# Two value products side by side, and two differential scores side by side, in the attention of a two-layer hybrid trunk

## The reference

```python
h = x @ w_in
q_lat, ckv, krope, g_mla, dq, dk, dv, g_diff = _split_cols(h, EVEN_SECTIONS)

# latent attention: one softmax map a head, values from the compressed latent
s = einsum('bqhc,bkc->bhqk', q_abs, ckv) + einsum('bqhr,bkr->bhqk', q_rope, krope)
p = softmax(where(_chunk_mask(qpos, kpos), s * MLA_QK_DIM ** -0.5, NEG_INF))
o_lat = einsum('bhqk,bkc->bqhc', p, ckv)        # then times w_uv, head by head

# differential attention: two maps a head, the second subtracted
s = einsum('bqhid,bkhid->bhiqk', dq, dk) * DIFF_HD ** -0.5      # DIFF_HD = 64
p = softmax(where(_chunk_mask(qpos, kpos), s, NEG_INF))
a = p[:, :, 0] - lam * p[:, :, 1]
o_diff = einsum('bhqk,bkhe->bqhe', a, v)

o = concatenate([o_mla * silu(g_mla), rmsnorm(o_diff) * silu(g_diff)]) @ w_out
y = layernorm(ALPHA * x + o)
```

## Time and profile before

| | us |
|---|---|
| median of 3 runs | 844.55 (844.47 to 845.53) |
| the profiled execution, its own time | 844.67 |
| its span, first to last instruction | 842.9 |
| TensorE busy | 813.1 (96%) |
| VectorE busy | 524.9 (62%) |
| ScalarE busy | 412.1 (49%) |

### The profile page before, as it was taken

The page is one execution under the profiler, slowest core; times in us unless marked ns, Lnnn a source line. Parts: engine busy times, 40 slices in busy tenths (PEclk is TensorE's granted clock), DMA queues, the critical chain, the costliest instruction groups (busy, mean ns, idle before and its releaser), DMA issues.

```text
span 842.9 us, 17104 instructions
## 1 busy us (share of the span) xinstructions
PE 813.1 (96%) x6676; PEld 707.9 (84%) x6676; DVE 524.9 (62%) x1045; ACT 412.1 (49%) x945; POOL 74.8 (9%) x102
## 2 busy tenths in 40 slices
PE   6999999999999999999999999999999999999995
PEld 6996688888888899778899998888988888887674
DVE  4265355665665657766942565666577676778877
ACT  4233533334444456532324555675566665687710
POOL 2120000100000000000310010001100110121002
PEclk9999999999999999999999999999999999999998
DMA  7631211211323334514133334333332333334103
GB/s 234 153 97 50 75 44 52 64 49 42 121 77 105 112 97 134 158 61 137 57 124 109 114 101 140 92 106 110 128 101 91 127 126 115 117 125 132 60 30 125
DMA packets 67533, 86.25 MB, mean 102 GB/s; under 512 B 6016, under 2 KB 53920, under 8 KB 67456
## 3 DMA queue, kind: packets, MB, share of 16 engines
q1 hardware_dynamic: 63712, 74.47, 28.7%
q0 software_dynamic: 3744, 10.70, 4.0%
HBM read 74.25 MB, written 10.90 MB: 101 GB/s over the span
## 4 chain that ended last, share of the span: by engine, by line
PE 80%; issue 9%; DVE 5%; ACT 4%; POOL 2%; DMA 1%; SPq 0%; DVEq 0%; POOLq 0%; ACTq 0%
PE turn L955 24%; PE pair L955 17%; PE value L955 16%; PE proj L955 15%; PE turn L995 3%; PE turn L1171 2%; POOL rstd L928 1%; PE value L995 1%; PE proj L995 1%; PE proj L1171 1%; DVE w_lo L1604 1%; ACT w_hi L1371 1%; DMA x_sb<-in_x_prompt_dram 1%; PE pair L995 1%; DVE probs L1719 0%
## 5 line engine op out<-in xcount | busy, mean ns | idle before, releaser
L1604 DVE TENSOR_TENSOR w_lo<-stage,w_hi 128x512 fp32r<-128x512 f32 (+1 forms) x136 | 91.9, 682 | 114.4 <-ACT w_hi L1371 114.0
L955 PE MATMUL turn<-w_hi,xT_hi 128*128 128x256 f32 (+2 forms) x340 | 106.0, 312 | 1.0 <-DVE xT_lo L1609 0.7
L955 PE MATMUL turn<-w_hi,xT_lo 128*128 128x256 f32 (+2 forms) x340 | 102.5, 301 | 0.0
L955 PE MATMUL turn<-w_lo,xT_hi 128*128 128x256 f32 (+2 forms) x340 | 102.4, 301 | 0.0
L1371 ACT CAST w_hi<-stage 128x512 fp32r<-128x512 f32 (+1 forms) x144 | 87.4, 616 | 19.2 <-PE value L955 6.5
L955 PEld LDWEIGHTS turn<-w_hi,xT_hi 128*128 128x128 f32 x340 | 64.8, 191 | 3.7 <-DVE x_sb L1851 1.5
L955 PEld LDWEIGHTS turn<-w_hi,xT_lo 128*128 128x128 f32 x340 | 64.8, 191 | 2.5
L955 PEld LDWEIGHTS turn<-w_lo,xT_hi 128*128 128x128 f32 x340 | 64.9, 191 | 2.1
L1451 ACT ACTIVATE work<-pair,peak 128x512 f32<-128x512 f32 (+4 forms) x80 | 40.9, 516 | 46.2 <-DVE peak L1708 46.1
L1719 DVE TENSOR_TENSOR_SCAN probs<-probs 128x512 f32<-128x512 f32 (+4 forms) x80 | 61.4, 801 | 1.6
L955 PE MATMUL value<-w_hi,xT_hi 128*128 128x256 f32 (+2 forms) x194 | 60.1, 310 | 0.7 <-DVE w_lo L1604 0.7
(11 more groups left out here) (535 smaller groups left out, 2079.6 us busy)
## 6 DMA issues: line engine op xcount, KB each, us to landing
stage<-in_w_in_odd_dram SPq DMA_DIRECT2D x64, 256.0 KB, 2.7
stage<-in_w_in_even_dram SPq DMA_DIRECT2D x44, 256.0 KB, 2.8
k_c<-in_cache_sb_k_dram SPq DMA_DIRECT2D x32, 256.0 KB, 3.5
v_c<-in_cache_sb_v_dram SPq DMA_DIRECT2D x32, 256.0 KB, 2.9
mlaK<-in_cache_diff_k_dram SPq DMA_DIRECT2D x8, 512.0 KB, 4.1
mlaK<-in_cache_diff_v_dram SPq DMA_DIRECT2D x8, 512.0 KB, 4.5
stage<-in_w_out_even_dram SPq DMA_DIRECT2D x16, 256.0 KB, 2.6
stage<-in_w_out_odd_dram SPq DMA_DIRECT2D x16, 256.0 KB, 2.6
```

The lines of the kernel that those rows point to most:

```text
L955: return nc.tensor.matmul(o, l, r, start=first, stop=last)
L1604: v.tensor_tensor(piece(w_lo[:, sec % 2, words]), piece(stage[:, n % STAGES, :]), piece(w_hi[:, sec % 2, words].bitcast(F32)), ALU.subtrac ...
```

## The change

Two edits of the list, and one helper in TensorE's code.

- "value" of the first latent prompt step of a two (M 3 or M 2) is put off by one turn. It then stands directly ahead of the "value" of its neighbour (M 0 or M 1). There are eight such twos.
- Where two differential prompt steps stand next to each other (`firsts`: D (3, 0), (3, 3), (2, 1), (2, 3), (1, 1) and (0, 2)), the 64-row products of both come first (two jobs "rows"), then the masks of both, all at the first step's turn. The second step's score is thus a turn earlier. The code of the products is moved into `diff_scores`; the number of products does not change. The order on VectorE, ScalarE and SyncE follows the list.

```diff
--- before.py
+++ after.py
@@ -72,13 +72,24 @@
     def weighted(s):
         return [("turn", s)] + ([("turn2", s)] if s[0] == "M" else [])
 
+    heads = [i for i, s in enumerate(steps) if s[0] == "D"]
+    firsts = [i for i in heads if i + 1 in heads and (heads.index(i) == 0 or i - 1 not in heads)]
+
+    def values(i):
+
+        kinds = steps[i][0] + steps[i + 1][0] if i + 1 < len(steps) else ""
+        return [] if kinds == "MM" else [i - 1, i] if i and steps[i - 1][0] + steps[i][0] == "MM" else [i]
+
     for i, now in enumerate(steps):
-        jobs.append(("score", now))
+        if i in firsts:
+            jobs += [("rows", now), ("rows", steps[i + 1]), ("score", now), ("score", steps[i + 1])]
+        elif i - 1 not in firsts:
+            jobs.append(("score", now))
         between = fills.get(i, [])
         if now[0] == "MS":
             jobs += flat_jobs(between)
-        if i >= 3:
-            s = steps[i - 3]
+        for n in values(i - 3) if i >= 3 else []:
+            s = steps[n]
             jobs.append(("value", s))
             for turns_on, job in after(s):
                 later.setdefault(i + turns_on, []).append(job)
@@ -995,6 +1006,16 @@
                     i = nc.tensor.transpose(ps(job)[0:c, c0:c0 + r], src, ident[0:r, 0:r])
                 i.then_inc(filled[where[job][0]], 1)
 
+            def diff_scores(s):
+
+                _, t, h = s
+                for j in range(t + 1):
+                    wait_drained(pe, ("dkT", j, h // 2))
+                wait_drained(pe, ("dqT", t, h // 2))
+                for i in range(2):
+                    r = slice(HD * i, HD * i + HD)
+                    mm(ps(("score", s))[:, i, 0:width(s)], dqT[t][r, h, :], dkT[r, h, 0:width(s)], True, False)
+
             pe.wait_ge(consts_in, 16)
             for job in schedule:
                 kind = job[0]
@@ -1073,11 +1094,15 @@
                     pe.wait_ge(kc_in[b % 2], 16 * (4 * g + b // 2 + 1))
                     transposes(job, [((2 * i + half) * P, k_c[:, b % 2, half, i * P:(i + 1) * P])
                                      for i in range(2) for half in range(2)])
+                elif kind == "rows":
+                    wait_bank(pe, ("score", job[1]))
+                    diff_scores(job[1])
                 elif kind == "score":
                     s = job[1]
                     n = width(s)
-                    wait_bank(pe, job)
                     o = ps(job)
+                    if ("rows", s) not in schedule:
+                        wait_bank(pe, job)
                     if s[0] == "M":
                         _, t, pair = s
                         pe.wait_ge(kr_done, PT_TILES)
@@ -1104,13 +1129,8 @@
                         mm(o[:, 0:PAST], qrb, kr_cT[0:QK, b % 2, :], False, False)
                         mm(o[:, PAST:n], qrb, krTs[0:QK, b * NEW:(b + 1) * NEW], False, True).then_inc(done, 1)
                     elif s[0] == "D":
-                        _, t, h = s
-                        for j in range(t + 1):
-                            wait_drained(pe, ("dkT", j, h // 2))
-                        wait_drained(pe, ("dqT", t, h // 2))
-                        for i in range(2):
-                            r = slice(HD * i, HD * i + HD)
-                            mm(o[:, i, 0:n], dqT[t][r, h, :], dkT[r, h, 0:n], True, False)
+                        if ("rows", s) not in schedule:
+                            diff_scores(s)
                         for i in range(2):
                             m = mm(o[:, i, n - P:n], identb[:, :], mask_chunk[:, :], False, True)
                         m.then_inc(done, 1)
```

## The result

The changed kernel takes 838.82 us (four runs, 837.91 to 839.20) against 844.51 before (844.47 to 845.53): ratio 0.9928, 95% interval 0.9911 to 0.9945. Run again beside the experiments it took 838.05 against 844.54, ratio 0.9925 (0.9913 to 0.9938). It is faster, by 5.7 and by 6.5 us. Forecast were 840.0 and a gain of 4.6.

The account below looks back on a forecast made before the run. TensorE, busy for 96% of the span, was taken to bound the kernel. Terms of 1.84, 0.43, 1.56 and 0.73 sum to 4.56 us off the median 844.55, forecasting 840.0 us, range 838.6 to 842.3.

Parts of the forecast that it names:

- borders of eight value visits: Latent value products: eight twos each save one entry to and exit from 64-column weights, 0.23 us each, 1.84 us.
- wait at the first visit: First round, value of M (3, 0): its wait for VectorE's copy of its transposed weights goes, 0.43 us.
- waits of four light steps: Ends of M (0, 1), M (0, 2), M (1, 2), M (1, 3): put-off values fill TensorE's idle time before sample scores, 1.56 us.
- scores of six twos: Differential scores: paired steps save way in and slow product behind masks, 0.15 us in each of four twos; 0.73 us in all.
- so this stays: Transposes behind a value visit: the first one's 0.16 us instead of 0.11 was taken to remain, as behind masks.
- hangs on a chain: Light step M (0, 1): VectorE's last cache copy was said to follow the last projection through ScalarE's copy, rotation and weights' conversion.
- There I find nothing that becomes late: Full steps: a projection of 2.9 us stands before every such need, so no time change was counted.
- The 0.85 stays: Score (2, 0), 384 columns: its four 64-row products were to take 0.85 us in the new place too.
- it is paid inside the mode as well: Differential 64-row products: some 0.1 us of uncovered weight load in each pass was to remain without a mode change.
- It does more: Rival: passes hide the other step's load, 0.2 us in six twos, and the holes vanish in full; 838.6 us, chance 0.08.
- Given back: Rival: TensorE reaches something later that is not tied to it, such as a transfer, and waits; about 844.5 us, chance 0.05.
- VectorE's backlog: Slower rival, differential part: delayed first scores and queued maxima hold up the copy of transposed weights; 847.0 us, chance 0.04.

Follow-up runs that it names:

- the runs with the early copy: Cache transposes one job earlier: in the kernel before, 841.24 us; with values also two by two and differential scores alone, 838.89 us.
- the early copy: Kernel before, with the transposes of a latent sample's cache one job earlier, ahead of the weights' conversion: 841.24 us against 844.80.
- the doubled products: Kernel before, with the 64-row products of the six paired and the other differential prompt steps issued twice in a row: 852.24 us.
- the repetition: The changed kernel measured once more, unedited, beside the experiments: 838.05 us, 0.9925 of the kernel before.
- the second layer's paired scores: Changed kernel, with scores of neighbouring prompt steps in the second layer's groups 0 to 2 also sharing 64-row products and masks (12 twos): 888.70 us.

## Why the prediction was right or wrong

| step | forecast | shown |
|---|---|---|
| borders of eight value visits | 1.84 | 8 x 0.29 = 2.3 (2.55 from the runs with the early copy) |
| wait at the first visit | 0.43 | 0.43 |
| waits of four light steps | 1.56 | 1.56 |
| bank waits of two full steps | none | 0.74 |
| scores of six twos | 0.73 | 1.7 |
| sum | 4.56 | 6.7, of 6.95 by the trace |

- **Borders.** The mechanism was right, the size short by 0.06 a visit (0.09 by the runs with the early copy, where four twos gave 0.30 and four 0.34). The step that failed is "so this stays": I took the slow first transpose to come behind masks as it does behind a value visit. In after it doesn't; only the products with attention weights pay it behind masks. I had laid a price of one shape on another.
- **Light steps.** Right in sum, if a little less at M (0, 1) and M (0, 2) (0.37 for 0.44) and more at M (1, 2) and M (1, 3) (0.41 for 0.34). But one sentence was wrong: that the copy "hangs on a chain". It was ready 0.6 us before, behind a conversion in VectorE's queue; moving it by one job gave the whole gain (2.05 us at these four steps) without any pairing.
- **Full steps.** "There I find nothing that becomes late" failed because something was late already, and by luck of the bank rotation the wait went: 0.74 us for a term that the forecast put at nothing. That it is this copy, the early copy shows (0.35 and 0.37 at the same two places). That the change removed it by giving the cache another bank is read from the names in the two traces; no run changed the bank alone.
- **Scores.** The step that failed is "The 0.85 stays", and "it is paid inside the mode as well". The 0.2 us above the rate of full-array products are not 0.1 for each pass: one 0.1 stands between the first pass and the second, the other before the masks, and a step that comes second inside the mode pays neither, as the doubled products show. I had divided a total by two passes and had no third pass to compare with. The four twos in the middle gave 0.36, 0.36, 0.36 and 0.32, where I had 0.15; the first 0.31, where I had 0.08; the last 0.06, as forecast (0.05). The sum that I set aside, 0.15 + 0.2 a two "with each pass's 0.1 laid to the change of mode", was the right one. It builds on what the Trainium skill's page "TensorEngine Tiling (Array Packing)", Key Properties, says of a change of mode, and the trace agrees that going in and out costs (0.09 and 0.105, and 0.10). The 0.105 comes back after a stop inside the mode as well, so it does not hang on the change alone. The sentence of the Trainium skill's page "TensorE: Matmul & The Clock Gate", Part 3, on which I leaned for the smaller sum, that a load of weights overlaps running products only when its row group differs, does not fit this trace: with both row halves at work, 512 columns take 422 ns from pass to pass, 106 for 128 of them, the rate of full-array products (109), so the loads of the later passes cost nothing that can be seen.
- **Rivals.** "It does more" was the nearest (838.6 for 838.8 and 838.1), and the size of its first half, 0.2 a two, is what was shown for five twos of six; its second half, holes that vanish, isn't. At 0.08 it stood too low. "Given back" had a small part too: the wait for a transfer took 0.52 us in the repetition's profile. No bank held the products of (3, 1) back, as forecast from the earlier trace rows: TensorE's row there takes 1.92 us to the masks at 227.55, which is 7 + 527 + 7 + 422 + 7 + 422 + 8 + 521 ns. Nor did VectorE's backlog show: TensorE is idle for 1.5 us of the differential part in after as in before (135.00 less 133.53, 136.00 less 134.53).

```profile
225.63 1.99 PE L966 MATMUL pair<-dkT,x_sb 64*128 64x512 f32 x8
227.55 0.40 PE L966 MATMUL pair<-mask_chunk,identb 128*128 128x128 bf16 x4
```

## What to carry to other kernels

A change of array shape has a price for each stay, not for each product, and a stop inside the stay brings part of it back, so put work of one shape together; but first ask in which bank the pulled-up product lands and who reads that bank last. What won 0.3 us a two in the softmax lost 50 / 12 = 4 us a two in stick-breaking. Look for waits by the distance between starts, since modelled ends hid 0.37 us here; and where an engine waits for a copy, see what stands ahead of the copy in its queue before covering the hole. Rotating buffers hand out such waits by chance: after any move, look which job got the bank of the slow copy.

## What the runs showed of the hardware

- A stay in 64-row float32 products costs 0.09 us on the way in, 0.105 between the first and second pass and 0.10 before the masks behind; every other pass runs at the rate of its columns (422 ns for 512, 316 for 384, 209 for 256, 105 for 128). A stop of 1.2 to 2.7 us inside the mode brought the 0.105 back, at all eleven such stops of the second layer's paired scores.
- A stay in 64-column value products costs 0.09 in, 0.05 for the first pair (154 ns for 103) and 0.09 out, with 0.05 on the first full-array transposes behind.
- The start of the kernel scatters: the 25th product of the projections, ahead of which all these lists agree, started between 14.3 and 16.5 us in the fourteen profiled executions. That is as much as most of these edits are worth; for them the aligned traces tell more than the medians.
- The two transfers of the cache `ckv_c`, 128 KB each, that are issued between 135 and 160 us landed in 2.4 to 2.6 us in before and in the two runs that keep its order of values and scores, and in 3.0 to 3.3 in all the others, and TensorE came to wait for one. Why they took longer stays open; over all eight such transfers the median is 2.7 to 2.9 in every kernel.
